# Sparse attention scores with all 128 rows: GpSimd clears the other head's rows of each query block

## The reference

```python
def one_block(args):                     # Q_BLOCK = 128 queries
    qb, qib, wb, tb = args
    ...
    top_val, top_idx = lax.top_k(score, topk)
    k_sel = k[b_ar, top_idx]
    v_sel = v[b_ar, top_idx]
    s = jnp.einsum('bqhd,bqkhd->bqhk', qb, k_sel).astype(jnp.float32) * (dh ** -0.5)
    s = jnp.where(jnp.isfinite(top_val)[:, :, None, :], s, -jnp.inf)
    p = jax.nn.softmax(s, axis=-1).astype(v.dtype)
    return jnp.einsum('bqhk,bqkhd->bqhd', p, v_sel)
```

## Time and profile before

| | us |
|---|---|
| median of 3 runs | 3700.86 (3700.54 to 3710.74) |
| the profiled execution | 3704.7 |
| its span, first to last instruction | 3702.9 |
| TensorE busy | 3548.4 (96%) |
| DVE busy | 2023.2 (55%) |
| GpSimd busy | 1930.3 (52%) |
| ScalarE busy | 1008.3 (27%) |

### The profile page before, as it was taken

How to read it: one execution, slowest core, us unless ns; L and a number is a source line. 1 busy time by engine, 2 the same in 40 slices (tenths; PEclk the granted TensorE clock), 3 DMA queues, 4 the chain that set the end, 5 groups by cost and what they waited for, 6 DMA issues and landing times.

```text
span 3702.9 us, 44229 instructions
## 1 busy us (share of the span) xinstructions
PE 3548.4 (96%) x16768; PEld 2893.1 (78%) x16768; DVE 2023.2 (55%) x2958; ACT 1008.3 (27%) x1670; POOL 1930.3 (52%) x1177
## 2 busy tenths in 40 slices
PE   7999998989999999999898999989999999999998
PEld 6888776878888888876687888867778787777887
DVE  5553697636542454269653554057576525766641
ACT  2120246232110111024623211035433203533310
POOL 5666451436666666644143666631266663236664
PEclk9999999999999999999899999999999999999999
DMA  3323381312233223337031223344122235412232
GB/s 133 97 94 94 96 193 35 127 56 92 97 97 98 97 97 93 100 104 180 29 131 49 94 97 99 95 124 121 40 97 97 88 100 145 114 49 89 97 97 85
DMA packets 106684, 362.43 MB, mean 98 GB/s; under 512 B 14304, under 2 KB 14720, under 8 KB 105856
## 3 DMA queue, kind: packets, MB, share of 16 engines
q1 hardware_dynamic: 91648, 319.41, 26.9%
q0 software_dynamic: 8640, 31.46, 4.6%
q10 hardware_dynamic: 6208, 8.92, 0.9%
HBM read 317.27 MB, written 2.10 MB: 86 GB/s over the span
## 4 chain that ended last, share of the span: by engine, by line
PE 71%; DVE 12%; issue 6%; ACT 6%; DMA 3%; POOL 2%; ACTq 1%; DVEq 0%; SPq 0%; POOLq 0%
PE banks L553 23%; PE banks L554 23%; PE banks L555 23%; DVE diagonals L920 2%; DMA w_raw<-mid 1%; DVE h_lo L902 1%; DVE square_sum L677 1%; ACT probs L983 1%; DVE squares L924 1%; ACTq L647 1%; DMA w_lo<-w_raw 1%; DVE w_lo L594 1%; ACTq L646 1%; ACT diagonals L889 1%; ACT probs L977 1%
## 5 line engine op out<-in xcount | busy, mean ns | idle before, releaser
L589 POOL CAST w_hi<-w_raw 128x1024 fp32r<-128x1024 f32 (+1 forms) x540 | 563.6, 1044 | 1404.0 <-PE banks L555 1297.1
L594 POOL TENSOR_TENSOR w_lo<-w_raw,w_hi 128x1024 fp32r<-128x1024 f32 (+1 forms) x508 | 1235.8, 2433 | 40.6
L553 PE MATMUL banks<-h_hi,w_hi 128*128 128x512 f32 x2928 | 1161.4, 397 | 49.9 <-DVE h_lo L902 21.3
L554 PE MATMUL banks<-h_lo,w_hi 128*128 128x512 f32 x2928 | 1147.7, 392 | 0.0
L555 PE MATMUL banks<-h_hi,w_lo 128*128 128x512 f32 x2928 | 1146.9, 392 | 0.0
L553 PEld LDWEIGHTS banks<-h_hi,w_hi 128*128 128x128 f32 x2928 | 554.4, 189 | 185.9 <-issue 44.7
L555 PEld LDWEIGHTS banks<-h_hi,w_lo 128*128 128x128 f32 x2928 | 554.2, 189 | 117.9
L554 PEld LDWEIGHTS banks<-h_lo,w_hi 128*128 128x128 f32 x2928 | 554.9, 190 | 111.8
L553 PE MATMUL banks<-act_hi,w_hi 128*128 128x512 f32 x1056 | 411.9, 390 | 5.2 <-DVE act_lo L930 4.2
L555 PE MATMUL banks<-act_hi,w_lo 128*128 128x512 f32 x1056 | 411.5, 390 | 0.0
L554 PE MATMUL banks<-act_lo,w_hi 128*128 128x512 f32 x1056 | 411.3, 390 | 0.0
(11 more groups left out here) (391 smaller groups left out, 4335.6 us busy)
## 6 DMA issues: line engine op xcount, KB each, us to landing
w_raw<-gu SPq DMA_DIRECT2D x176, 512.0 KB, 3.5
w_raw<-mid SPq DMA_DIRECT2D x120, 512.0 KB, 3.5
w_raw<-up SPq DMA_DIRECT2D x88, 512.0 KB, 3.5
w_raw<-dn SPq DMA_DIRECT2D x96, 448.0 KB, 3.3
w_raw<-mix SPq DMA_DIRECT2D x62, 512.0 KB, 3.5
w_lo<-w_raw POOLq DMA_DIRECT2D x50, 512.0 KB, 5.1
w_raw<-dn SPq DMA_DIRECT2D x48, 512.0 KB, 3.5
w_raw_third<-mid SPq DMA_DIRECT2D x10, 512.0 KB, 5.0
```

The costliest lines, as they stand in the source:

```text
L553: pe.matmul(out, w_hi, m_hi, start=start, stop=False, skip_group_check=True)
L554: pe.matmul(out, w_hi, m_lo, start=False, stop=False, skip_group_check=True)
L589: g.tensor_copy(wh[:, ch.slot, 0:width], raw_tile(ch, width)).then_inc(Ring.hi[ch.slot], 1)
L594: eng.tensor_tensor(wl[:, ch.slot, 0:width], raw_tile(ch, width), f32(wh[:, ch.slot, 0:width]), ALU.subtract).then_inc(Ring.split[ch.slot], 1)
```

## The change

Before each score GpSimd writes a copy of the query block in which the rows of the other head of the tile are multiplied by 0 and those of its own head by 1 (`halfcol` holds the two columns of ones and zeros), once for the high and once for the low part. TensorE then takes this copy with all 128 rows of the key tile; the other head's keys meet zeros. The copies have four slots each (`q_slot`), in memory that held `square_sum` and the free end of `diagonals`. Item i may be written once the score of item i-2 is done. GpSimd writes items 0 to 13 behind its visit of chunk 27, 14 to 20 behind chunk 28, 21 to 27 behind chunk 29 and 28 to 31 behind chunk 30.

```diff
+    qz_hi = place("qz_hi", [4, P], F32R, at=ssum_at)
+    qz_lo = place("qz_lo", [4, P], F32R, at=dg_at + 3 * S * 4)
...
+    qz_s = sig("q_padded", 2 * HEADS * T)
...
+    def q_slot(h, t):
+        return 2 * (h % 2) + t % 2
...
         def scores(h, t, out):
-            r, q = head_rows(h), slice(t * P, (t + 1) * P)
             n = (t + 1) * P
...
-            return mm3(pe, out[:, 0:n], qk_hi[r, 4 + h // 2, q], qk_lo[r, 4 + h // 2, q], qk_hi[r, h // 2, 0:n],
-                       qk_lo[r, h // 2, 0:n], True, True)
+            pe.wait_ge(qz_s.sem, qz_s(l, 2 * (T * h + t + 1)))
+            z = q_slot(h, t)
+            return mm3(pe, out[:, 0:n], qz_hi[:, z, :], qz_lo[:, z, :], qk_hi[:, h // 2, 0:n], qk_lo[:, h // 2, 0:n],
+                       True, True)
...
+    def q_padded(g, l, i):
+        h, t = i // T, i % T
+        q = slice(t * P, (t + 1) * P)
+        if h % 2 == 0 and t == 0 and h < 4:
+            g.wait_ge(prope.sem, prope(l, 10 * (h // 2 + 1)))
+        elif h % 2 == 0 and t == 0:
+            g.wait_ge(rope1.sem, rope1(l, 15 + 10 * (h // 2 - 1)))
+        if i >= 2:
+            g.wait_ge(dsa.score.sem, dsa.score(l, i - 1))
+        for tile, full in ((qz_hi, qk_hi), (qz_lo, qk_lo)):
+            g.tensor_scalar(tile[:, q_slot(h, t), :], f32(full[:, 4 + h // 2, q]), halfcol[:, h % 2:h % 2 + 1], None, ALU.mult)\
+                .then_inc(qz_s.sem, 1)
+
+    PADDED_AT = {OUT_CHUNK + 2: (0, 14), OUT_CHUNK + 3: (14, 21), OUT_CHUNK + 4: (21, 28),
+                 OUT_CHUNK + 5: (28, HEADS * T)}
+
     def beside_top_k(g, l, m):
 
+        if m in PADDED_AT:
+            for i in range(*PADDED_AT[m]):
+                q_padded(g, l, i)
```

More of the change, by code:

```diff
@@ L191, in program @@
     probs = place("probs", [4, S], at=sq_at)
+    ssum_at = top[0]
     ssum = place("square_sum", [S])
+    dg_at = top[0]
     dg = place("diagonals", [2, 8, P])
+    qz_hi = place("qz_hi", [4, P], F32R, at=ssum_at)
+    qz_lo = place("qz_lo", [4, P], F32R, at=dg_at + 3 * S * 4)
     one = place("one", [4])
```

## The result

The changed kernel takes 3738.53 us (median of 4 runs, 3732.55 to 3740.84), the kernel before 3702.13 with one run more than when the forecast was made. The ratio is 1.0088, 95% interval 1.0069 to 1.0106: slower, as forecast, but by 36.4 us between the medians (33 by the ratio, 26 to 39 by its interval) for the +15.8 of the sum, and outside the range of 3709 to 3728. The profiled execution is one of the four; its span is 3739.0 us, 36.1 more than the one of before.

A forecast was written before the change was run, and what follows sets the result against it. DVE and ScalarE's loop bounds the stage's middle; TensorE is one link in the start's chain. Late start 14.4 plus splits 1.4 gave +15.8 us: 3720.5 profiled, 3716.7 as median, range 3709 to 3728.

The forecast's parts named there:

- Direction and start: Start of the sparse attention stage: score 0 behind GpSimd's chunk 27 visit delays the first exponential 7.2 us a layer, +14.4.
- rival 2: Stage start: TensorE's clock stays high, +11.5+1.4 = +12.9 us, 3713.8; chance 0.26.
- The clearing: GpSimd's 128x128 product, two per item: 0.38 us each, 0.76 an item, hidden in the middle of the stage.
- my middle bounds: GpSimd product of 128 columns: 0.29 us from its casts, 0.48 from its two-input subtractions.
- The splits: Items 14, 21, 28 behind splits of chunks 28 to 30: 6.7 us of TensorE waits a layer, 0.7 coming through.
- I put the first two at 0: Waits before scores 14 and 21 cost nothing; only the wait at item 28 costs, 0.7 us a layer, +1.4.
- Rival 3: Splits of chunks 28 to 30 cost full price: 13.4 us replaces 1.4, total +27.8, 3728.7; chance 0.10.
- 128 rows: Scores: no row-mode changes saves TensorE 0.3 us an item, 19 us, but gains 0 because DVE and ScalarE set the middle.
- Rival 1: All 64 items: TensorE sets the pace, each gaining up to 0.4 us; -14 us, 3687; chance 0.07.
- GpSimd and DVE: Rotary steps: the engines get in each other's way, each costing one clearing, 15 us more, 3732; chance 0.06.
- cheap clearings: Stage start: GpSimd products of 0.29 us instead of 0.38, 0.4 us less a layer, -0.8 in all.
- the last term: End of the stage: TensorE's catch-up after item 28's late split, 0.7 us a layer, +1.4.

The follow-up runs named there:

- the run with the start's wait only: Kernel before, score 0 of each layer waiting for a one-column memset on GpSimd's queue behind chunk 27; no clearings, 64-row products: 3719.65 us, 1.0034.
- the run with the clearings alone: Changed kernel with all 128 clearings, but scores computed from 64 rows as before without waiting for them: 3708.39 us, 1.0006.
- the waits alone: Kernel before, scores 14, 21 and 28 waiting for memsets behind the splits of chunks 28, 29 and 30; no clearings: 3715.42 us, 1.0029.
- the four loops with the waits alone: Two layers each of two runs on the kernel before: waits at scores 14, 21, 28 (1.0029), and those plus score 0 (1.0078).
- the wait before score 16: Changed kernel, two more clearings ahead of each split: 3722.08 us; also with items 0 and 1 cleared behind chunk 24, 3718.08, or chunk 22, 3715.81.
- the run without subtractions: Changed kernel, only blocks of items 0 and 1 cleared, early, used by all 128-row scores; subtractions for chunks 28 to 30 replaced by memsets: 3709.46 us, 1.0008.
- 128 rows alone: Changed kernel, only blocks of items 0 and 1 cleared, early, and used by every 128-row score; subtractions kept: 3714.50 us, 1.0027.
- with both: Kernel before, scores 0, 14, 21 and 28 waiting for memsets on GpSimd's queue; no clearings, 64-row products: 3733.96 us, 1.0078.

## Why the prediction was off

**Direction and start: right.** The change moved score 0 behind GpSimd's transfer of chunk 27, and the mean, DVE, ScalarE and all items with it. Forecast 7.2 us a layer, 14.4 in all; measured 9.0 and 8.6, 17.6. The mechanism stands alone in the run with the start's wait only. Its size was low by 1.8 and 1.4 us, and the terms show where: four clearings to score 1 are 2.8 us (560.79 to 563.59) for 1.52+0.06, and the mean 3.62 for 3.2. The low clock was taken rightly (0.51 from 558 to 568), which lets rival 2 fall.

**The clearing: mis-sized.** 0.38 us forecast, 0.60 measured, above both of my middle bounds (0.29 and 0.48): 128 columns cost as much as the best cast of 512 columns, 0.61, so the line through casts of 512 and 1024 columns doesn't reach down to small tiles. It costs the start 0.9 us a layer and is hidden in the loop, as the run with the clearings alone shows.

**The splits: the step that failed.** "I put the first two at 0 … +1.4." The loops grew by 6.25 and 7.51 us, 13.8 together, and the waits alone, without a clearing, gave 10.7 us. The forecast let 6.7 us of waits a layer (1.8, 2.0 and 2.9) go in and 0.7 come out. What goes in was larger than that, in two parts.

First, the low clock behind the waits. I priced it at the start and put it at nothing here. In the changed kernel it lasts 10.2 us in layer 0 and 13.7 in layer 1, which takes 5.1 and 6.8 us of TensorE's work. That it costs time by itself is shown by the four loops with the waits alone and by the wait before score 16.

Second, the waits are longer: 2.70, 2.47 and 3.68 in layer 0, 8.9 (layer 1: 9.0) for 6.7. About half a microsecond of each is the longer clearings. The split is released by TensorE itself, three chunks back. From the start of the cast to the moment at which TensorE is ready for score 14 it is 2.90 us in before (593.37 to 596.27), 2.69 in after (603.48 to 608.87-2.70) and 2.98 with the waits alone (597.29 to 601.29-1.02): a faster TensorE brings the split and the score forward together, so it doesn't shorten the wait.

What was let absorb them was not too much. Waits and lost clock are 14.0 and 15.8 us a layer (an estimate from the rows), and the loops grew by 6.25 and 7.51, so some 8 us a layer were covered, where the forecast let 6.0 be covered. With 64-row products, in the run with the waits at the splits alone, it was 2 to 3 us: the lead. The rest fits the 0.3 us an item that 128 rows save, 6 us over the twenty items; this is an estimate, no run takes it apart. What does show it: with 128 rows and nothing to wait for at the splits TensorE has free time in the middle (it has work for 44.7 of the 50 us from 588 to 638 in the run without subtractions, and waits 4.9 us for DVE; 48.9 of 50 in before).

Rival 3 had the waits as the cost, its full price of 13.4 and a time of 3728.7, at a chance of 0.10. That 13.4 meets the 13.8 is luck: it stood for waits without any cover, and there was cover and the low clock besides.

**128 rows: right at 0 as a gain.** The 0.33-us steps are gone and 0.3 us an item is saved. It is a saving on an engine that has to follow another one's loop: it makes nothing faster, and in the changed kernel it seems to have paid for part of the waits. The Trainium skill ("TensorEngine Tiling (Array Packing)", Key Properties) says that a change of tiling mode drains TensorE. The rows agree: the longer steps are there with 64 rows and gone without. Rival 1 falls with the loop of 48.86 us in the run in which TensorE had every chance.

**GpSimd and DVE: another place than forecast.** Not the 64 clearings, which cost 1.0006, but three subtractions per layer decide, and by timing: none of it on the path in before, 2.5 us a layer with 128 rows alone. In the changed kernel the step from head 2 to 3 is 11.19 us for 9.91, with a 2.51-us rotary product and the 2.70-us wait in the same item; how much belongs to which wasn't separated. The Trainium skill ("SBUF — State Buffer", Who interferes with whom) has DVE operations with two SBUF inputs contend with GpSimd's that read SBUF, one of the two standing still for the other's whole instruction; the product that ended 0.55 us after the subtraction agrees.

**The sum.** Forecast 14.4+1.4 = 15.8. By the profile 17.6+13.8 = 31.3 (before rounding) and 5 elsewhere that I don't explain; by the runs with one part each 12.6 (start) and 10.7 (splits), with both 29 (24 to 34) for the changed kernel's 33 (26 to 39). Two slips in the forecast's own arithmetic change nothing: rival 2 with cheap clearings and the last term at 0 comes to 3711.6, not 3710.7 (still under 3712.0, and only with both), and 2.9-1.8-0.5 is 0.6, not 0.7.

## What to carry to other kernels

When a new wait is put on an engine, ask what releases the thing it waits for. If that is the engine's own progress, being faster doesn't shorten the wait, and it comes at every occurrence; more work between release and use does (with two items more between them, two of three waits were gone). An engine that has work all the time in a stretch can't make up for a wait there even if another engine sets the pace: here its lead paid for some 2 us. And price each wait with the low-clock stretch that may come behind it: an equal wait of 2.7 us cost 0.6 us without it and up to 3.5 with it.

## What the hardware showed that I had not expected

A GpSimd instruction beside a dense DVE stream may be held for as long as the stream lasts, or hardly at all. DVE's convolution issues a product with two SBUF inputs every 0.66 us. The same 128x128 clearing in this stream took 1.20 us in one kernel, 4.63 in another and 16.50 in a third (0.98 and 1.40 at the same place in layer 1 of two of them). All three long ones (16.50, 4.63 and 4.34) ended 0.44 or 0.45 us after DVE had begun the addition that closes the stream (line 1638, at 554.36, 532.27 and 1727.12), the first instruction of it to start 0.78 us behind the one before and not 0.66. What decides whether a clearing gets in at once I have not settled: the 16.50 began 0.03 us ahead of a DVE product (538.31, 538.34), the 1.20 began 0.02 us behind one (537.34, 537.32). While clearings got through, DVE's products took 0.86 for 0.74 us.

GpSimd's multiplication of 128x128 elements took 0.60 us, as much as its cast of 128x512 at best (0.61).

Nothing in a kernel's own edit needs to touch two engines for them to collide: taking 0.3 us an item off TensorE moved a GpSimd instruction by 1 us relative to DVE, and that cost 2.5 us a layer.
